# Half of each up product's inner length as seven block products

## The reference

```python
h = rms_norm(h_res, norm_mlp_g[i])
h_res = h_res + jnp.square(jax.nn.relu(h @ w_up[i])) @ w_down[i]     # w_up 2048 x 8192, w_down 8192 x 2048
out = rms_norm(h_res, final_norm_g)
```

## Time and profile before

| | |
|---|---|
| median of 3 runs | 2339.45 us (2339.33 to 2339.72) |
| the profiled execution | 2340.56 us, span 2338.8 us |
| mean granted clock of TensorE | 0.998 |
| TensorE busy | 2317.7 us, 99% of the span |
| VectorE, ScalarE, GpSimd busy | 1494.2, 1020.2, 299.8 us |
| chain that ended last | PE 93%, of it dense products (line 1902) 42% of the span |
| in 977 to 2332 us | the MLP: eight groups, 167.7 us from up half to up half |

### The profile page before, as it was taken

One profiled execution on the slowest core, in us unless ns is written; L12 is line 12 of the kernel. 1 busy time (PEld: TensorE's weight loads), 2 busy tenths in 40 slices (PEclk: granted clock), 3 DMA queues, 4 the chain that ended last, 5 costly groups with the idle time before them and its releaser, 6 DMA issues.

```text
span 2338.8 us, 49871 instructions
## 1 busy us (share of the span) xinstructions
PE 2317.7 (99%) x18736; PEld 2086.8 (89%) x18736; DVE 1494.2 (64%) x2366; ACT 1020.2 (44%) x1836; POOL 299.8 (13%) x340
## 2 busy tenths in 40 slices
PE   8999999999999999999999999999999999999998
PEld 8999999999999788789889889889889799899888
DVE  7558668567577654558558458467467476475356
ACT  6534434434344422435435345345345354354336
POOL 5102011011012132101001001001001001001007
PEclk9999999999999999999999999999999999999999
DMA  8244243343443643636526527437447347347434
GB/s 252 75 109 96 74 108 80 99 98 80 98 105 92 182 135 94 185 91 136 150 77 155 141 78 170 128 91 171 115 101 176 99 104 171 98 118 195 121 112 141
DMA packets 513328, 286.43 MB, mean 122 GB/s; under 512 B 84510, under 2 KB 490528, under 8 KB 512672
## 3 DMA queue, kind: packets, MB, share of 16 engines
q1 hardware_dynamic: 478512, 224.19, 34.7%
q0 software_dynamic: 24064, 56.20, 11.8%
q10 hardware_dynamic: 10496, 2.62, 0.6%
HBM read 232.47 MB, written 50.47 MB: 121 GB/s over the span
## 4 chain that ended last, share of the span: by engine, by line
PE 93%; DVE 3%; DMA 3%; issue 1%; SPq 0%; ACT 0%; ACTq 0%; DVEq 0%
PE PD L1902 42%; PE PD L1907 18%; PE PW L2178 6%; PE PW L2180 6%; PE PW L2179 6%; PE PD L2178 2%; PE PD L2180 2%; PE PD L2179 2%; PE PD L2121 1%; PE PD L1931 1%; PE PW L1931 1%; DMA w_raw<-in_w_in 1%; PE PW L1981 1%; DMA gram<-NA 1%; PE PW L2081 1%
## 5 line engine op out<-in xcount | busy, mean ns | idle before, releaser
L1902 PE MATMUL PD<-act_lo,w_hi 128*128 128x512 f32 x1344 | 531.5, 395 | 0.0
L1902 PE MATMUL PD<-act_hi,w_hi 128*128 128x512 f32 x1344 | 529.4, 394 | 1.5 <-issue 1.5
L1902 PE MATMUL PD<-act_hi,w_lo 128*128 128x512 f32 x1344 | 528.5, 393 | 0.0
L2178 PE MATMUL PW<-form_hi,w_hi 128*128 128x256 f32 x1120 | 312.6, 279 | 0.0
L2180 PE MATMUL PW<-form_hi,w_lo 128*128 128x256 f32 x1120 | 312.6, 279 | 0.0
L2179 PE MATMUL PW<-form_lo,w_hi 128*128 128x256 f32 x1120 | 312.6, 279 | 0.0
L1902 PEld LDWEIGHTS PD<-act_hi,w_hi 128*128 128x128 f32 x1344 | 252.5, 188 | 63.9 <-issue 3.0
L1902 PEld LDWEIGHTS PD<-act_hi,w_lo 128*128 128x128 f32 x1344 | 252.8, 188 | 57.3
L1902 PEld LDWEIGHTS PD<-act_lo,w_hi 128*128 128x128 f32 x1344 | 252.1, 188 | 57.9 <-issue 0.2
L1352 DVE TENSOR_TENSOR w_lo<-w_raw,w_hi 128x512 fp32r<-128x512 f32 x268 | 207.4, 797 | 107.7 <-ACT w_hi L931 104.3
L931 ACT CAST w_hi<-w_raw 128x512 fp32r<-128x512 f32 x268 | 160.3, 620 | 250.8 <-DMA w_raw<-in_w_in 104.0
(11 more groups left out here) (378 smaller groups left out, 4085.4 us busy)
## 6 DMA issues: line engine op xcount, KB each, us to landing
w_raw<-in_w_in SPq DMA_DIRECT2D x200, 256.0 KB, 3.2
w_raw<-in_w_down SPq DMA_DIRECT2D x136, 256.0 KB, 3.1
w_more<-in_w_down SPq DMA_DIRECT2D x136, 256.0 KB, 3.1
w_raw<-in_w_up SPq DMA_DIRECT2D x128, 256.0 KB, 3.2
w_more<-in_w_up SPq DMA_DIRECT2D x128, 256.0 KB, 3.4
residual<-delta POOLq DMA_DIRECT2D x56, 512.0 KB, 5.8
w_raw<-in_w_out SPq DMA_DIRECT2D x64, 256.0 KB, 2.8
residual<-res POOLq DMA_DIRECT2D x4, 2048.0 KB, 10.1
```

The source lines that it names most:

```text
L1902: ins = M(pd_seq(n)[:, 0:width], w, v[:, k, first:first + width], start=begin, stop=end)
L2178: M(bank_for(product, p), whi, hi, start=begins and k == 0, stop=False, skip_group_check=True)
```

## The change

An up pair (tiles u and u + 4) is now one unit. Of its inner length, quarters 0 and 2 (k-tiles 0 to 3 and 8 to 11) become a 2 x 2 block product of seven products with 256 columns, as in the down half; quarters 1 and 3 stay plain (`PLAIN`), but are done per half of the tokens, 256 columns. Both accumulate in the same banks. The forms of h are made once, behind the output tiles 8 to 11, by ScalarE and VectorE (`forms_of_h`); they take the place of half of `act_hi` and `act_lo`.

The unit now has seven products and four plain blocks, each with one ring slot: 11 splits where 8 stood. The ring for the MLP has 5 slots (RM), high and low at different places; freed room holds forms, sums and raw blocks. For pair 0 of a group, and for the down half, VectorE sums weight blocks; for pairs 1 to 3 GpSimd does (`sum_blocks(u, g)`), three additions a pair. The third sum now overwrites the second.

ScalarE keeps p1, p5, p6, p7 of an up pair (`keep_up`), VectorE adds the banks to them (`gather`, five operations of 256 columns) before it scales. The token sums stand behind p5 of the first pair, in bank 2 of PD; before the last dense product TensorE waits for all gathers. The residual is read back in three transfers into room of `act_both`.

```diff
+SUM_IN = {"p5": 1, "p6": 2, "p3": 2, "p7": 0}
 SUM_STEP = {"p5": 1, "p7": 1, "p6": 2, "p3": 3}
+FREED_BY, FREED_BY_POOL = (2, 2, 5, 5), (4, 2, 5, 6)
...
+GATHERED_0, N_GATHERED = 1, 5
+KS = KT // 4
+H_STEP = (2, 2, 1, 1, 3, 4, 4)
+PLAIN = ((0, 1), (0, 3), (1, 1), (1, 3))
+R_PAIR, L_PAIR = NP + len(PLAIN), len(BLOCKS) + len(PLAIN)
+R_UP, L_UP = R_PAIR * HALF_UT, L_PAIR * HALF_UT
...
+RM = 5
+N_UNITS = HALF_UT + HALF_KT
+HI_AT, LO_AT = (4, 0, 1, 2, 3), (4, 5, 6, 7, 3)
...
+        def sum_blocks(u, g):
+
+            first = L_PAIR * u
+            raw = w_raw if first % RAW_MLP == 0 else w_more
+
+            def loaded(name):
+                rel = first + BLOCKS.index(name)
+                pool.wait_ge(raw_loaded[rel % RAW_MLP], at(raw_sum(rel), 16 * L_GROUP // RAW_MLP, g))
+
+            def made(count):
+                pool.wait_ge(sum_made, at(3 * u + count, 3 * N_UNITS, g))
+
+            for name in ("a11", "a21", "a22"):
+                loaded(name)
+            pool.wait_ge(lo_split, at(Q_MLP + R_PAIR * (u - 1) + NP, R_GROUP, g))
+            flat = lambda ap: ap.rearrange("p s k n -> p s (k n)")
+            nc.gpsimd.tensor_tensor(flat(w_sum01[:, 0:2]), flat(raw[:, 1:2]).to_broadcast([P, 2, KQ * P]), flat(raw[:, 0:3:2]),
+                                    ALU.add).then_inc(sum_made, 1)
+            made(1)
+            nc.gpsimd.tensor_tensor(w_sum(2), raw[:, 0], w_sum(1), ALU.add).then_inc(sum_made, 1)
+            loaded("a12")
+            made(2)
+            pool.wait_ge(lo_split, at(Q_MLP + R_PAIR * u + PRODUCTS.index("p6") + 1, R_GROUP, g))
+            nc.gpsimd.tensor_tensor(w_sum(2), raw[:, 3], w_sum(2), ALU.add).then_inc(sum_made, 1)
+
         with pool.Fori(0, FFG - 1) as g:
+            for u in range(1, HALF_UT):
+                sum_blocks(u, g)
...
+        pool.dma_start(res_a[:], res_view[:, 0:7, :]).then_inc(res_back, 16)
+        pool.dma_start(res_b[:], res_view[:, 7:14, :]).then_inc(res_back, 16)
+        pool.dma_start(res_c, res_view[:, 14:16, :]).then_inc(res_back, 16)
+        for u in range(1, HALF_UT):
+            sum_blocks(u, FFG - 1)
+        pool.wait_ge(quarter_used, Q_LAST)
...
+            act.wait_ge(quarter_used, at(Q_MLP + i - RM + 1, R_GROUP, it))
+            nc.scalar.copy(hi_slot(i), w_sum(SUM_IN[product]) if rel is None else raw_mlp(rel)).then_inc(hi_split, 1)
...
+        def gain_h(k):
+
+            if k:
+                act.wait_ge(h_ready, 4 * k)
+            for h, made in ((0, form[:, 0::NP, :]), (1, form[:, 2:4, :])):
+                tile = k + KT // 2 * h
+                act.wait_ge(evacuated[(T_OUT + tile) % 2], free(T_OUT + tile))
+                nc.scalar.activation(made, two(res[:, tile, :]), ACT.Copy, scale=p_("g_mlp", tile)).then_inc(gain_made, 1)
+
+        def round_h(k, step_, first, last):
+            act.wait_ge(h_made, 4 * k + step_)
+            nc.scalar.copy(h_forms(k)[:, 0, first:last, :], form[:, first:last, :]).then_inc(h_hi_ready, 1)
+
+        def forms_of_h(k):
+            gain_h(k)
+            act.wait_ge(gain_made, 2 * (k + 1))
+            nc.scalar.copy(h_forms(k)[:, 0, 2:4, :], form[:, 2:4, :]).then_inc(h_hi_ready, 1)
+            round_h(k, 1, 0, 2)
+            round_h(k, 2, 4, 5)
+            round_h(k, 4, 5, 7)
...
+        def keep_part(unit, place, product, scale, e, free_when, g):
+
+            act.wait_ge(quarter_used, at(Q_MLP + e + 1, R_GROUP, g))
+            semaphore, count, per = free_when
+            act.wait_ge(semaphore, at(count, per, g))
+            nc.scalar.activation(part[:, place, :], bank_for(product, unit), ACT.Copy, scale=scale).then_inc(part_kept, 1)
...
+            def next_slot(u, i):
+                if i == 0:
+                    act.wait_ge(form_made, at(4 * u + 4, 4 * HALF_UT, g))
+                    round_forms(u, 5, 7)
+                if i == 1:
+                    keep_next(u, 1, g)
+
+            for u in range(HALF_UT):
+                for i in range(R_PAIR):
+                    if u and i in (0, 1):
+                        split_mlp(R_PAIR * u + i + RM, g)
+                        next_slot(u - 1, i)
+                        continue
+                    if i < NP:
+                        keep_up(u, i, g)
+                    split_mlp(R_PAIR * u + i + RM, g)
+                    if i == NP + 1:
+                        square(u, 0)
+                        act.wait_ge(form_made, at(4 * u + 1, 4 * HALF_UT, g))
+                        round_forms(u, 0, 2)
+                    if i == NP + 3:
+                        square(u, 1)
+                        act.wait_ge(u_sq, at(2 * u + 2, UT, g))
+                        round_forms(u, 2, 4)
+                        keep_next(u, 0, g)
+                        act.wait_ge(form_made, at(4 * u + 2, 4 * HALF_UT, g))
+                        round_forms(u, 4, 5)
...
+        def split_mlp(i, it=0, after=None):
+
+            shift, unit, product, rel = slot_use(i)
+            by_dve = not 0 < unit < HALF_UT
+            if product == "p1" and by_dve:
+                sum_blocks(i, 0, it, after)
             dve.wait_ge(hi_split, at(Q_MLP + i + 1, R_GROUP, it))
-            r = (Q_MLP + i) % RING
-            V.tensor_tensor(w_lo[:, r], src, w_hi[:, r].bitcast(F32), ALU.subtract).then_inc(lo_split, 1)
-            if product in ("p1", "p5"):
-                sum_blocks(p, 1 if product == "p1" else 2, it)
-
-        def sum_blocks(p, which, it):
-
-            raw = raw_pair(p)
+            V.tensor_tensor(lo_slot(i), w_sum(SUM_IN[product]) if rel is None else raw_mlp(rel), hi_slot(i).bitcast(F32),
+                            ALU.subtract).then_inc(lo_split, 1)
+            if product == "p1" and by_dve:
+                sum_blocks(i, 1, it)
+            if product == "p6" and by_dve:
+                sum_blocks(i - PRODUCTS.index("p6"), 2, it)
...
+                if after:
+                    dve.wait_ge(quarter_used, after)
...
+        def low_h(k, step_, first, last):
+
+            dve.wait_ge(h_hi_ready, 4 * k + step_)
+            V.tensor_tensor(h_forms(k)[:, 1, first:last, :], form[:, first:last, :], h_forms(k)[:, 0, first:last, :].bitcast(F32),
+                            ALU.subtract).then_inc(h_ready, 1)
+
+        def forms_of_h(k):
+            dve.wait_ge(gain_made, 2 * (k + 1))
+            V.tensor_tensor(t1, b11, b12, ALU.subtract).then_inc(h_made, 1)
+            low_h(k, 1, 2, 4)
+            dve.wait_ge(h_made, 4 * k + 1)
+            V.scalar_tensor_tensor(t2, t1, -1.0, b22, ALU.mult, ALU.subtract).then_inc(h_made, 1)
+            low_h(k, 2, 0, 2)
+            dve.wait_ge(h_made, 4 * k + 2)
+            V.tensor_tensor(t4, t2, b21, ALU.add).then_inc(h_made, 1)
+            V.tensor_tensor(t3, b22, b12, ALU.subtract).then_inc(h_made, 1)
+            low_h(k, 3, 4, 5)
+            low_h(k, 4, 5, 7)
...
+            if a >= 8 - RM:
+                split_mlp(a - 8 + RM, after=Q_MLP - 1)
+            if a in (5, 7):
                 for k in range(4 * (a - 4), 4 * (a - 3)):
-                    dve.wait_ge(act_hi_ready, KT + k + 1)
+                    dve.wait_ge(act_hi_ready, KT + plain_index(k) + 1)
                     V.scalar_tensor_tensor(act_lo[:, k, 0:SEQ], res[:, k, :], p_("g_mlp", k), act_hi[:, k, 0:SEQ].bitcast(F32),
                                            ALU.mult, ALU.subtract).then_inc(act_ready, 1)
...
+        def gather(u, i, g, b_at):
+
+            add_part = lambda place, bank: V.tensor_tensor(b_at[place], bank, part[:, place, :], ALU.add).then_inc(gathered, 1)
+            if i == NP - 1:
+                dve.wait_ge(part_kept, at(4 * u + 4, 4 * N_UNITS, g))
+                V.scalar_tensor_tensor(part[:, 3, :], bank_for("p7", u), -1.0, part[:, 3, :], ALU.mult, ALU.add).then_inc(gathered, 1)
+            if i == NP + 1:
+                dve.wait_ge(quarter_used, at(Q_MLP + R_PAIR * u + i + 1, R_GROUP, g))
+                add_part(0, bank_for("p2", u))
+                add_part(1, bank_for("p3", u))
+                dve.wait_ge(gathered, at(GATHERED_0 + N_GATHERED * u + 3, N_GATHERED * HALF_UT, g))
+            if i == NP + 3:
+                dve.wait_ge(quarter_used, at(Q_MLP + R_PAIR * u + i + 1, R_GROUP, g))
+                add_part(2, bank_for("p4", u))
+                add_part(3, PD[:, 0, 0:NEAR])
+                dve.wait_ge(gathered, at(GATHERED_0 + N_GATHERED * u + 5, N_GATHERED * HALF_UT, g))
+
+        def scale(made):
+            V.scalar_tensor_tensor(made, made, 0.0, two(rs1[:]), ALU.max, ALU.mult).then_inc(scaled, 1)
...
+            b_at = (b11, b12, b21, b22)
+            for u in range(HALF_UT):
+                for i in range(R_PAIR):
+                    if i == NP + 1:
+                        if u:
+                            dve.wait_ge(form_ready, at(4 * u, 4 * HALF_UT, g))
+                        else:
+                            for h in range(2):
+                                dve.wait_ge(delta_added[h], at(16, 16 * HALF_KT // 2, g))
```

(96 more changed lines are left out.)

522 lines of the change are left out of this document (274 added, 248 removed).

## The result

The changed kernel takes 2342.76 us, median of 20 runs (2340.66 to 2346.83); the kernel before takes 2339.72 us beside it (one of its 20 runs took 5857.67 us, the others 2338.25 to 2342.05). The ratio is 1.0015, 95% interval 1.0008 to 1.0021: no gain, 0.15% slower. The forecast was 2305 us, "faster" with 0.88. So some 38 us have to be found, in a kernel that does multiply fewer columns. In what follows, the tile hf holds the forms of h, act_both the plain quarters, and uf the forms that the down half reads. The profiled execution has a span of 2342.8 us at a mean granted clock of 0.995.

What follows compares the result with a forecast made beforehand. TensorE's stream of matmuls was taken to bound the kernel: 40.9 us saved, less 5.2 at the MLP's start and 1.1 at its end, gives 34.6 off 2339.45, forecast 2305 us. Range 2300 to 2322 us.

Steps and rivals of the forecast that it cites:

- The duration of a 256-wide matmul: In the MLP's up pairs and down half, 0.1168 us against 0.2323 for 512 wide, ratio 0.503.
- Both 0: GpSimd's first sum behind transfers, in the first group (residual store) and last group (delta, read-backs), costs TensorE nothing.
- The start: From the out-projection's end (X), TensorE waits for VectorE's square and p3's split: 5.2 us more, bounds 2 and 8.
- TensorE at X+29: First group: GpSimd's sum ends near X+20, TensorE wants it only at X+29, X being the out-projection's end; cost 0.
- The end: Before the last dense product TensorE waits for both additions of the last gather: 1.1 us.
- Seams: Between two up pairs no stall, with 0.3 to 0.5 us to spare; bounds 0 to 16 us over 32 seams.
- GpSimd's price: A 1024-wide weight sum on GpSimd takes 2.4 us, three sums 5.0 us a pair, none late.
- the lock's order: At the first plain quarter VectorE's split starts before GpSimd's sum, so no stall: 0, bounds 0 and 10 us.
- rivals 1 and 2: 1: seams or GpSimd's lock stall pairs, 2311 to 2329, chance 0.20; 2: GpSimd locks first at dearest price, 2353, chance 0.06.
- Rival 3: 256-wide matmuls dearer in the plain part, where two banks alternate: 0.127 us each, 2361 us, chance 0.02.
- signs of being wrong: A pair over 21.4 us, TensorE waiting at the first plain quarter, or the start losing over 10 us.
- what the change takes off TensorE: Up pairs: 22.30 us becomes 21.02, 1.28 saved a pair, 40.9 us over 32 pairs.

Runs made afterwards that it cites:

- m_rate: TensorE alone, 46 streams of 96 matmuls differing only in where operands lie: 0.1167 us at the old forms' places, 0.1183 at act_both's.
- a_place: Changed kernel with act's low parts and uf's first two inner tiles moved 32 bytes: 2328.02 us, ratio 0.9951.
- e_noloop: Changed kernel with TensorE's loop over the seven groups written out: ratio 0.9957, 13.6 us less than the changed kernel.
- m_place: TensorE alone in the changed kernel's own order, 36 placings of act and hf with five of uf: the kernel's own placing takes 21.25 us a pair.
- c_place: Changed kernel with loop written out, last group's waits and start's order moved, store and read-backs spread, and 32-byte tile shifts: 2301.63 us, ratio 0.9838.
- b_noloop: Kernel before with TensorE's loop over the groups written out, nothing else: 2339.41 us, ratio 0.9990.
- m_class: TensorE alone, streams with hi and lo offsets within 128 bytes set one by one, an offset-32 stream behind each: 0.1133 to 0.1200 us a matmul.
- e_delta: Changed kernel with VectorE's last-group delta wait moved later and GpSimd's pair 1 sums ahead of its delta wait and read-backs: ratio 1.0000, 3.5 us less.
- e_start: Changed kernel with earlier square of the last out tile, later reciprocal, and GpSimd's first sums ahead of its store wait: ratio 0.9995, 4.7 us less.

## Why the prediction was wrong

The forecast took 38 us too little. By its steps:

- **The duration of a 256-wide matmul failed: a mis-sized term.** "That is 0.2323 us for a 512-wide and 0.1168 us for a 256-wide matmul: half the width costs half" was right as a reading and wrong as a constant. It set a wide matmul at act's place against a narrow one at the old forms' place; at act's place m_rate has 0.1183 against 0.2311, 2.4% over half. A pair saves 22.30 - 21.25 = 1.05, not 1.28 us: 7 us over 32 pairs. And for the down half the prediction says "tiles and constants at other addresses and token sums in another bank add no instruction: 0". They add none, but the tiles at other addresses cost 1.40 us a group, 10 us. Together some 17 us; a_place gave back 15.
- **The loop's return was not priced.** The earlier trace rows was read as two gaps "that no engine caused" and left. They were the return's cost where 512-wide matmuls stand; in the changed kernel it is 10.7 us of gaps and 15.1 with what follows them, some 3 of that low clock (13.6 between the medians of e_noloop). The 0.2323 us holds some of it, too: without the loop an up half of before takes 88.97 us, not 89.21.
- **The last group failed: "Both 0".** GpSimd's sum was priced there, but VectorE's own wait for the last delta, at the head of its list for that group, was not looked at. It stood in the code before, where TensorE has no wait there; that eight slots and longer tiles covered it is argued, not shown. 4.0 us and the low clock; this up half took 92.3 us where 85.2 was forecast.
- **The start was right in its first term and short in its others.** The square was to end at X+6.3 and ended at X+6.6 (X = 962.5); p3 was to start at X+13.9 and started at X+14.1. That TensorE would run at the low clock behind the first wait was missing. The store was taken to land 10.1 us behind its issue; GpSimd's wait for it took 14.6, the sum ended at X+25 in place of X+20, and ScalarE, which waits for it in its list, kept the part that pair 1's p6 needs 2.4 us late. "TensorE at X+29" had looked at the sum's own user only, not at what is queued behind it. First up half 94.6 us against some 91.0.
- **The end was right**: 1.0 us where 1.1 was forecast.
- **Seams were right, GpSimd's price was right for a sum alone, the lock's order wrong without effect.** From 1000 to 2140 us TensorE waits for nothing but the loop, save two p6 that start some 0.2 us late. A 1024-wide sum takes 2.38 us alone, where 2.4 was forecast, 2.39 to 2.43 in five more of 24 cases and 2.7 to 2.9 in the others, beside VectorE; 512 takes 1.29 or 1.62:

```profile
L948 POOL TENSOR_TENSOR w_sum<-w_raw x24: 2384/2834/2902, 985.1 to 2195.4; 128x1024 f32<-128x1024 f32 x24
L951 POOL TENSOR_TENSOR w_sum<-w_raw,w_sum x24: 1293/1624/1632, 987.6 to 2198.1; 128x512 f32<-128x512 f32 x24
```

(min, median and max in ns.) GpSimd starts first, against what was said, and VectorE's three splits beside it take 4.45 us in place of 1.9:

```profile
1332.54 2.90 POOL L948 TENSOR_TENSOR w_sum<-w_raw 128x1024 f32<-128x1024 f32 x1 [6.73 <-DVE w_lo L1493]
...
1333.84 4.45 DVE L1493 TENSOR_TENSOR w_lo<-w_more,w_hi 128x512 fp32r<-128x512 f32 x3 [0.66 <-ACT w_hi L1035]
```

The first of them is still ready for the plain quarter. So rivals 1 and 2 did not happen. Rival 3 was right that the plain part is dearer, 0.1184 us, but that is 5 of the 17 us, and its reason doesn't hold: m_place, where a plain quarter stays in one bank, takes 0.1183. It is place and width, not alternating banks. The Trainium skill's rule behind it ("TensorE: Matmul & The Clock Gate", Back-to-back issue gap) would have made narrow matmuls cost far more than half; the trace has 0.1184 against half of 0.2323, 1.9% more.

None of the prediction's signs of being wrong showed: a pair takes 21.25 us (21.4 was the bound), no plain quarter waits, and the start loses 9.6 us (10). They looked at waits and at pairs; the down half, where most of the lost rate is, was taken as settled.

Summed against the forecast, in the profiled executions: rate 16.8 (8 up halves of 84.96 us for 84.08, as without the loop, and 7 down halves of 79.89 for 78.49), loop 15.1, last group 7.1 and first group 3.6 less 0.9 each that is rate, 0.8 behind the MLP; less 2.2 us by which the MLP began earlier (first matmul at 962.5 in place of 964.7; in the other runs of the changed kernel and its variants it is 961.7 to 964.5). That is 39.4 us for the 38.6 that are missing between the spans.

That the step "what the change takes off TensorE" was right in kind is shown by c_place, where these losses are undone and forms take the 0.1167 us that the prediction assumed: groups of 162.67 us (162.6 forecast), pairs of 21.07 (21.02). Against b_noloop, the kernel before without its loop's cost and with forms at the same 0.1167 us, it is 0.9990 - 0.9838 = 0.0152, or 35.6 us; 34.6 were forecast. That the totals agree so well is partly luck: in the two profiled executions the seven up halves behind the first give 32.0 us where 34.7 were forecast, while the first, whose start is mended beyond the forecast, gives 1.9 where none was, and c_place's MLP begins 4.0 us earlier.

## What to carry to other kernels

A matmul's time read from one tile is that tile's time, at that width: before it is used for a tile at another address, see where in a partition both operands lie, and when tiles have moved, compare the rate of a stretch that was not meant to change. When an edit makes the instructions in a queue shorter, a fixed cost that the longer ones covered, a loop's return or a wait at the head of a list, can come to light; list the waits that cost nothing before. And a wait ahead of an engine holds all that is queued behind it: price it by the first thing in that list that somebody needs.

## What the runs showed of the hardware

- Start-to-start distances of 256-wide float32r matmuls, each with its weight load, at a granted clock of 1.00: 0.1133, 0.1167, 0.1178 or 0.1200 us, with mixtures in between, by the operands' offsets within 128 bytes and by what ran before (m_class); 512 wide 0.2267 to 0.2333, so that at equal offsets the narrow one takes 0.99 to 1.06 of half the wide one. In m_rate, distances between operands that are multiples of 1024 bytes, and which slot the weights have, changed nothing.
- A loop's return on TensorE: gaps of 1.57 to 2.24 us with 256-wide matmuls around it (the changed kernel, e_delta, e_start, a_place), none to 1.2 us with 512-wide ones in a shorter loop (the kernel before).
- Of those 24 gaps, the ones of 1.91, 1.99, 2.06, 2.12 and 2.24 us had a stretch of some 16 matmuls at the low clock behind them (0.21 us each); another of 1.99 us and 18 of 1.57 to 1.88 us had none.
- Two 2 MB stores (e_start) or three read-backs (e_delta) beside weight loads: a 256 KB block, which lands 3.0 us behind its issue in the median, took 10.8 and 12.8 us, and GpSimd's sum stood 14.5 and 12.4 us until then.
